# Memory products scaled after the product, the rotary tables an FFN earlier, and another order of the latent panels

## The reference

```python
def memory_attention(q_mem, mem, mem_norm_g, w_mem_kv, g_q, g_k):
    q = rms_norm(q_mem.reshape(b, s, MEM_HEADS, MEM_HEAD_DIM), g_q)
    k, v = jnp.split(rms_norm(mem, mem_norm_g) @ w_mem_kv, 2, axis=-1)
    k = rms_norm(k.reshape(b, m, MEM_HEADS, MEM_HEAD_DIM), g_k)
    ...softmax(q k / 8) v...

for layer in range(2):
    if layer == 1:
        shared = shared_mla_kv(x, ...)          # latent keys and values, rotary key
    x = x + 0.5 * swiglu(rms_norm(x, norm_g[layer, 0]), ...)
    h = rms_norm(x, norm_g[layer, 1])
    # layer 0: short convolution, three gates; layer 1: mla_queries and causal attention
    x = x + concatenate([y_mix, memory_attention(...)]) @ w_out[layer]
    x = x + 0.5 * swiglu(rms_norm(x, norm_g[layer, 2]), ...)
```

## Time and profile before

| | us |
|---|---|
| median of the runs | 3041.64 (3040.64 to 3044.88) |
| the profiled execution | 3040.4 |
| its span | 3038.2 |
| TensorE busy | 2986.5 (98%) |
| VectorE busy | 1828.8 (60%) |
| ScalarE busy | 943.8 (31%) |
| GpSimd busy | 231.7 (8%) |

### The profile page before, as it was taken

The page is one execution under the profiler, slowest core; times in us unless marked ns, Lnnn a source line. Parts: engine busy times, 40 slices in busy tenths (PEclk is TensorE's granted clock), DMA queues, the critical chain, the costliest instruction groups (busy, mean ns, idle before and its releaser), DMA issues.

```text
span 3038.2 us, 36195 instructions
## 1 busy us (share of the span) xinstructions
PE 2986.5 (98%) x13373; PEld 2418.5 (80%) x13373; DVE 1828.8 (60%) x2405; ACT 943.8 (31%) x1279; POOL 231.7 (8%) x107
## 2 busy tenths in 40 slices
PE   8999999999999999999999999999999998999999
PEld 7787788788888887888787888887888875688887
DVE  8896565567766546554587655446554467665532
ACT  4643632333222222222223222222222235322222
POOL 0043240000000000000032000002000022000000
PEclk9999999999999999999999999999999999999999
DMA  4222223233322222223332222332223321122232
GB/s 146 97 93 81 68 97 117 67 103 105 97 97 97 97 97 88 96 95 105 113 107 70 90 97 97 104 104 95 92 97 104 104 87 63 35 90 97 97 104 97
DMA packets 79305, 287.55 MB, mean 95 GB/s; under 512 B 8992, under 2 KB 9248, under 8 KB 78816
## 3 DMA queue, kind: packets, MB, share of 16 engines
q1 hardware_dynamic: 77904, 280.06, 27.5%
q0 software_dynamic: 1296, 6.03, 0.6%
HBM read 283.96 MB, written 2.10 MB: 94 GB/s over the span
## 4 chain that ended last, share of the span: by engine, by line
PE 83%; issue 10%; DVE 5%; POOL 2%; ACT 1%; DMA 0%; POOLq 0%; ACTq 0%; DVEq 0%
PE ps L663 26%; PE ps L665 26%; PE ps L664 26%; POOL w_lo L622 2%; PE ps L1052 1%; PE ps L1297 0%; DVE w_lo L1846 0%; PE ps L1260 0%; DMA mem_x<-in_mem 0%; ACT w_hi L1344 0%; PE ps L833 0%; PE ps L727 0%; PE ps L1041 0%; DVE small L1997 0%; PE ps L947 0%
## 5 line engine op out<-in xcount | busy, mean ns | idle before, releaser
L1344 ACT ACTIVATE w_hi<-raw 128x1024 fp32r<-128x1024 f32 x524 | 554.4, 1058 | 1385.7 <-PE ps L665 1383.5
L663 PE MATMUL ps<-h_hi,w_hi 128*128 128x512 f32 (+1 forms) x2379 | 935.1, 393 | 8.7 <-DVE w_lo L1846 3.3
L665 PE MATMUL ps<-h_hi,w_lo 128*128 128x512 f32 (+1 forms) x2379 | 924.3, 389 | 0.0
L664 PE MATMUL ps<-h_lo,w_hi 128*128 128x512 f32 (+1 forms) x2379 | 924.3, 389 | 0.0
L1846 DVE TENSOR_TENSOR w_lo<-raw,w_hi 128x1024 fp32r<-128x1024 f32 x434 | 530.7, 1223 | 473.9 <-ACT w_hi L1344 473.1
L663 PEld LDWEIGHTS ps<-h_hi,w_hi 128*128 128x128 f32 x2379 | 448.4, 188 | 115.7 <-issue 13.5
L665 PEld LDWEIGHTS ps<-h_hi,w_lo 128*128 128x128 f32 x2379 | 447.8, 188 | 93.0
L664 PEld LDWEIGHTS ps<-h_lo,w_hi 128*128 128x128 f32 x2379 | 448.2, 188 | 92.0 <-issue 2.6
L663 PE MATMUL ps<-mid_hi,w_hi 128*128 128x512 f32 x1208 | 470.8, 390 | 2.2 <-DVE mid_lo L1924 2.1
L664 PE MATMUL ps<-mid_lo,w_hi 128*128 128x512 f32 x1208 | 470.0, 389 | 0.0
L665 PE MATMUL ps<-mid_hi,w_lo 128*128 128x512 f32 x1208 | 470.0, 389 | 0.0
(11 more groups left out here) (409 smaller groups left out, 2471.7 us busy)
## 6 DMA issues: line engine op xcount, KB each, us to landing
raw<-in_wstream SPq DMA_DIRECT2D x525, 512.0 KB, 3.3
x<-in_x SPq DMA_DIRECT2D x4, 512.0 KB, 7.1
x_in<-in_x POOLq DMA_DIRECT2D x8, 256.0 KB, 3.2
mem_x<-in_mem POOLq DMA_DIRECT2D x2, 1024.0 KB, 5.1
out<-x SPq DMA_DIRECT2D x8, 256.0 KB, 4.5
tmp<-in_ret_decay POOLq DMA_DIRECT2D x1, 1024.0 KB, 5.0
rope_r<-in_rope_r POOLq DMA_DIRECT2D x1, 512.0 KB, 3.7
mats<-in_mats SPq DMA_DIRECT2D x1, 256.0 KB, 8.4
```

The source lines that it names most:

```text
L663: nc.tensor.matmul(dst, hi_w, hi_x, start=first, stop=False)
L664: nc.tensor.matmul(dst, hi_w, lo_x, start=False, stop=False)
L665: return nc.tensor.matmul(dst, lo_w, hi_x, start=False, stop=last)
L1344: nc.scalar.activation(w_hi[:, n % HL], raw[:, r], ACT.Copy).then_inc(hi_ready, 1)
```

## The change

1. The root of `mem` is applied behind the product: the halves are made of `mem` times its gain alone, the high one by ScalarE (`memory_hi`), the low one by VectorE (`memory_lo`, one step for a tile). In layer 0 VectorE drains the four memory tiles with a product with the root's reciprocal (`memory_drain`); in layer 1 ScalarE still drains them and VectorE scales them in place (`memory_scaled`).
2. The squares of `mem` are one ScalarE instruction, their sum one `tensor_reduce` of VectorE.
3. In norm round 0 the three scalings stand ahead of the tap `conv_part(st, 3, 1, 3)`.
4. The positions are loaded right behind `mem_x`, before GpSimd's run `conv0`; the rotary tables are computed by VectorE behind the first two units of `s0b_in`, and the Sin stands behind the Silus of `s0b_in`.
5. Latent order: the sums of `cq` stand behind the fourth panel of `mla_in`; the first two memory panels come first in `uq`, the query panel with one tile (number 4) before number 3; rounds 3 to 6 and the rotations move with them; the last round is spread behind the first scores.

```diff
-MEM1_PANEL, MEM1_TILE = (2, 3, 7, 8), (10, 11, 17, 18)
-UQ_PANEL, UQ_TILE = (0, 1, 4, 5, 6), (2, 3, 6, 7, 12, 13, 14, 15, 16)
-V_TILE = (0, 1, 4, 5, 8, 9)
+MEM1_PANEL, MEM1_TILE = (0, 1, 7, 8), (2, 3, 17, 18)
+UQ_PANEL, UQ_TILE = (2, 3, 4, 6, 5), (4, 5, 8, 9, 12, 13, 15, 16, 14)
+V_TILE = (0, 1, 6, 7, 10, 11)
...
@@ GpSimd @@
             pool.dma_start(mem_x[:], A["mem"]).then_inc(side_loaded, 16)
             pool.wait_ge(side_loaded, 48)
+            pool.dma_start(krope[:, 0].bitcast(I32), A["positions"].to_broadcast([P, S])).then_inc(side_loaded, 16)
+            pool.wait_ge(side_loaded, 64)
             split_run("conv0")
...
             pool.dma_start(mem_x1[:], A["mem"]).then_inc(side_loaded, 16)
-            pool.wait_ge(side_loaded, 64)
-            pool.dma_start(rope2[:, 0].bitcast(I32), A["positions"].to_broadcast([P, S])).then_inc(side_loaded, 16)
             pool.wait_ge(side_loaded, 80)
...
@@ TensorE, mla_in, ukv, uq @@
+                if j == 3:
+                    sums("cq")
...
                 if g == 0:
-                    sums("cq")
-                if g == 1:
                     spread_norms("cq")
...
             v_turned_tiles(0)
-            uq_gemm(0)
+            mem1_gemm(0)
+            mem1_gemm(1)
             round_spread(1)
             round_sums(2)
+            uq_gemm(0)
             v_turned_tiles(2)
+            round_spread(2)
+            round_sums(3)
             uq_gemm(1)
-            round_spread(2)
             v_turned_tiles(4)
-            mem1_gemm(0)
-            mem1_gemm(1)
+            round_spread(3)
+            turn(krope[:, 0])
             uq_gemm(2)
-            round_sums(3)
+            uq_gemm(4)
+            round_sums(4)
             uq_gemm(3)
-            round_spread(3)
-            round_sums(4)
-            uq_gemm(4)
             round_spread(4)
             round_sums(5)
-            turn(krope[:, 0])
             mem1_gemm(2)
+            normalised(4)
+            turn(q_rope[:, 0])
             round_spread(5)
             round_sums(6)
-            normalised(4)
-            turn(q_rope[:, 0])
             mem1_gemm(3)
-            round_spread(6)
-            memory_turned(st.t + MEM1_TILE[2] + 1, mem_vt1, 0)
...
             pair_scores(0)
             pair_scores(1)
-            memory_turned(st.t + MEM1_TILE[3] + 1, mem_vt1, 1)
+            round_spread(6)
+            for j in range(2):
+                memory_turned(mem_vt1, j, (mem_scaled, 3 + j))
...
@@ ScalarE @@
+                if n == ST["conv0"].n + 2:
+                    act.wait_ge(side_loaded, 48)
+                    nc.scalar.activation(mem_squares, mem_x[:], ACT.Square).then_inc(mem_squared, 1)
+                if n == ST["conv0"].n + 3:
+                    memory_hi(0, mem_x, mem_hi)
...
-            ffn("s0b")
+            silus("s0b_in", root)
+            act.wait_ge(sin_in, 2)
+            nc.scalar.activation(rope2, rope2, ACT.Sin).then_inc(sin_done, 1)
+            gemm("s0b_out", to_stage("s0b_out"), parts=3)
...
             v_copies(0)
-            uq_drain(0)
+            mem1_drain(0)
+            mem1_drain(1)
+            act.wait_ge(mem_scaled, 2)
+            round_squares(3, qm[:, 0], qm[:, 1], mem_k1_whole)
             round_root(2)
             aux[0] += 3
+            uq_drain(0)
             v_copies(2)
-            act.wait_ge(h_ready, 5 * DT)
+            round_root(3)
+            aux[0] += 4
             uq_drain(1)
             v_copies(4)
-            mem1_drain(0)
-            mem1_drain(1)
-            drained_up_to(MEM1_TILE[1])
-            round_squares(3, qm[:, 0], qm[:, 1], mem_k1_whole)
+            drained_up_to(UQ_TILE[3])
             uq_drain(2)
-            round_root(3)
-            aux[0] += 3
             drained_up_to(UQ_TILE[4])
             round_squares(4, *(q_rope[:, j] for j in range(3)))
-            uq_drain(3)
+            uq_drain(4)
+            drained_up_to(UQ_TILE[5])
+            round_squares(5, *(q_nope[:, hd] for hd in range(3)))
             round_root(4)
...
@@ VectorE @@
+            def memory_sum():
+                dve.wait_ge(mem_squared, 1)
+                v.tensor_reduce(acc[:, 0:MEM], mem_squares.rearrange("p k n -> p n k"), AX.X, ALU.add).then_inc(acc_ready, 1)
...
+            def memory_lo(l, mem, hi, lo, tiles):
                 for k in tiles:
-                    h = acc[:, MEM * (k % 2):MEM * (k % 2) + MEM]
-                    done(v.scalar_tensor_tensor(out=h, in0=mem[:, k], scalar=vcol("mem_norm_g_2", 8 * l + k),
-                                                in1=r[:, 0:MEM], op0=ALU.mult, op1=ALU.mult))
-                    halves(hi[:, k], lo[:, k], h, h_ready)
+                    dve.wait_ge(mem_cast, 8 * l + k + 1)
+                    v.scalar_tensor_tensor(out=lo[:, k], in0=mem[:, k], scalar=vcol("mem_norm_g_2", 8 * l + k),
+                                           in1=hi[:, k].bitcast(F32), op0=ALU.mult, op1=ALU.subtract).then_inc(h_ready, 1)
+
+            def memory_drain(j):
+                st = ST["mem0"]
+                dve.wait_ge(panel_done, st.n + j + 1)
+                dst = mem_k[:, j] if j < 2 else mem_vt[:, j - 2]
+                v.tensor_tensor(dst, bank(st.t + j)[:, 0:MEM], mem_root, ALU.mult).then_inc(drained, 1)
+
+            def memory_scaled(j):
+                dve.wait_ge(drained, ST["uq"].t + MEM1_TILE[j] + 1)
+                tile = mem_k1[:, j] if j < 2 else mem_vt1[:, j - 2]
+                v.tensor_tensor(tile, tile, mem_root, ALU.mult).then_inc(mem_scaled, 1)
...
-            conv_part(st, 3, 1, 3)
             round_norms(*memory_gain("q", 0), qm[:, 0], qm[:, 1])
             round_norms(*memory_gain("k", 0), mem_k_whole)
+            conv_part(st, 3, 1, 3)
...
+            def rotary_tables(c):
+                if c == 0:
+                    dve.wait_ge(side_loaded, 64)
+                    done(v.tensor_copy(angle, krope[:, 0].bitcast(I32)))
+                    done(v.tensor_scalar(angle, angle, vcol("inv_freq", 0), None, ALU.mult))
+                    rotary_table(0, 0.25)
+                if c == 1:
+                    rotary_table(1, 0.0)
+
+            ffn("s0b", gain2(1, 0), behind=rotary_tables)
...
+            memory_lo(1, mem_x1, mem1_hi, mem1_lo, range(4, 8))
             round_reciprocal(1)
-            memory_input(1, mem_x1, spare[:, 0], mem1_hi, mem1_lo, range(4, 8))
+            for j in range(2):
+                memory_scaled(j)
             round_norms(gk, *(k_nope[:, hd] for hd in range(3)))
```

More of the change, by code:

```diff
@@ L382, in build @@
         rope_in = [cpad[:, 0, 4:], cpad[:, 1, 4:], stage[:, 0], stage[:, 1]]
+        rope2, angle, turns = cpad[:, :, 4:], ckv[:, 0], ckv[:, 1]
         ret_out = [[stage[:, 0], stage[:, 1]], [cpad[:, 0, 4:], cpad[:, 1, 4:]]]
@@ L387, in build @@
         mem1_hi, mem1_lo = by_token(h_hi[:, 4:8]), by_token(h_lo[:, 4:8])
-        mem_k1, mem_v1 = (spare[:, j].rearrange("p (a n) -> p a n", n=MEM) for j in range(2))
-        mem_k_whole, mem_k1_whole = mem_k[:].rearrange("p a n -> p (a n)"), spare[:, 0]
+        mem_v1 = spare[:, 1].rearrange("p (a n) -> p a n", n=MEM)
+        mem_k_whole, mem_k1_whole = (k[:].rearrange("p a n -> p (a n)") for k in (mem_k, mem_k1))
+        mem_root = spare[:, 0, 0:MEM]
         mem_vt1 = rstd[:].rearrange("p (a n) -> p a n", n=MEM)
@@ L1697, in _ @@
                     root()
-                if n == ST["conv1"].n:
-                    memory_root(spare[:, 0])
-            def memory(l, k, v_in):
-                st = ST[f"mem{l}"]
-                for j in range(4):
-                    split(st.n + j + 1)
-                    if j == 0:
-                        act.wait_ge(drained, st.t)
-                    drain(st.n + j, st.t + j, k[:, j] if j < 2 else v_in[:, j - 2], cols=MEM)
-            memory(0, mem_k, mem_vt)
+                if n == ST["conv0"].n + 2:
[3 more added lines that the diff above has]
+                    memory_hi(0, mem_x, mem_hi)
+                if n == ST["conv1"].n:
+                    memory_root()
+            for j in range(4):
+                split(ST["mem0"].n + j + 1)
             act.wait_ge(drained, ST["mem0"].t + 2)
@@ L2541, in _ @@
                 scaled(ST["qm0"].n + j, ST["qm0"].t + j, qm[:, j])
-            memory_rms(r)
-            memory_input(0, mem_x, r, mem_hi, mem_lo, range(0, 4))
+            memory_rms()
+            memory_lo(0, mem_x, mem_hi, mem_lo, range(0, 4))
             conv_part(ST["conv1"], 2, 0, 2)
-            memory_input(0, mem_x, r, mem_hi, mem_lo, range(4, 8))
+            memory_lo(0, mem_x, mem_hi, mem_lo, range(4, 8))
             conv_part(ST["conv1"], 2, 1, 2)
@@ L2570, in _, with rotary_table @@
             x_gemm("wo0", residual(1.0, "wo0", gain2(0, 2)), 3)
-            ffn("s0b", gain2(1, 0))
+            magic = 1.5 * 2.0 ** 23
+            c1 = 6.28125
+            c2 = float(np.float32(np.round((2 * np.pi - c1) * 2.0 ** 20) / 2.0 ** 20))
+            c3 = 2 * np.pi - c1 - c2
```

(25 more changed lines are left out.)

87 lines of the change are left out of this document (33 added, 54 removed).

## The result

The changed kernel takes 3048.9 us (median of 12 runs, 3044.3 to 3050.7) against 3041.7 us of the kernel before beside it (12 runs, 3039.6 to 3044.9). The ratio is 1.0019, 95% interval 1.0011 to 1.0028, so 5.8 us slower (3.3 to 8.5); it is the ratio of the means, and the medians are 7.2 us apart. The twelve times stand in two groups with nothing between: five from 3044.3 to 3045.1, seven from 3048.9 to 3050.7. The profiled execution, 3044.5 us, is of the lower one.

The account below looks back on a forecast made before the run. TensorE, busy 2986.5 of 3038.2 us, was taken as the bound. The terms 5.0 + 7.5 - 3.65 - 4.8 - 4.7 = -0.65, from the median 3041.6, gave 3041.0 us, range 3033 to 3048.5.

Parts of the forecast that it names:

- A: conv0: GpSimd waits at once for the positions' load before its low halves; 5.0 us slower, ends 2 and 5.8.
- B: s0b: rotary tables on VectorE delay its low halves, two waits of TensorE; 7.5 us slower, ends 5.5 and 10.
- C: First memory product: VectorE reaches the panels in time but for 0.95 us; 3.65 us faster, ends 1.5 and 4.9.
- E: MLA stage: 14.5 us of losses go, 9.8 of new waits come; 4.7 us faster, ends 0 and 12.2.
- D: First norm round: scaling ahead of a tap removes TensorE's wait for mem_k; 4.8 us faster, ends 3 and 5.
- E's first wait: MLA stage, between the two first memory panels: TensorE waits 3.65 us for GpSimd's low half, plus 1.3 of clock.
- F: Rival, MLA stage: weights for the second memory panel and uq panel 3 come in time; 3033.5 us, chance 0.20.
- S: Rival, MLA rounds: VectorE and GpSimd block each other, costing 8 us; 3049 us, chance 0.14.
- N: Rival, first memory product: VectorE still arrives late at the second panel, gain there 0; 3044.7 us, chance 0.08.

Follow-up runs that it names:

- A alone: Kernel before, with only a second load of the positions in front of GpSimd's conv0 run, waited for there: 3048.6 us, ratio 1.0019.

## Why the prediction was wrong

The forecast was 3041.0 with a range up to 3048.5; the median is 3048.9, and slower by more than 0.2% had 0.16 of the chance, within 0.2% 0.62, and the ratio, 1.0019, is at that edge. Of the 7.9 us between forecast and median, 4.7 lie in the profiled execution (3039.8 forecast, 3044.5 measured) and 3.2 between it and the median.

- **The waits: right.** A 3.72 us (forecast 3.72); B 3.58 and 2.37 (3.75 and 2.4); C 0.77 (0.95); the two in front of MLA panels 3.72 and 2.23 (3.65 and 2.55). E's others: 0.78 for the sums (0.5), 1.09 and 0.71 for a reciprocal and the rotation's tile (0.8 and 0.95); unforeseen are 0.78 in front of the last ukv panel and 0.47 at 2561, both for ScalarE's drains. GpSimd's first half in conv0 began at 1517.01.
- **C and D: right in size,** -3.6 and -5.4 in the profile; D was taken back by itself and cost 6.4 us. C wasn't run alone.
- **The step that failed is the price of the clock:** "I price a new wait of over 2.8 us at its length plus 1.3, a shorter one at its length." The waits of 2.37 and 2.23 us, priced at their length, had 1.3 and 1.5 us of half clock behind them; the wait of 1.88 us in front of s1a_out, with none behind it in the trace of before, had 1.1. The long ones had 1.7, 1.7 and 1.5 instead of 1.3. That is 4.9 us of half clock over the forecast, nearly all of the 5.2 by which the profiled span missed the sum; the waits not foreseen and D's better result make up most of the rest. The evidence for "none behind the waits of about 2 us" was one execution of before. In ten of fourteen profiles the 1.9 us of s1a_out are followed by half clock, and that trace was one of the four others. The size was misread too: 2.05 is half of a window whose granted clock was 0.58, so by that clock 1.7 us were lost in it.
- **A second term was too small, the step from the profile to the median.** The forecast added 1.2 us from the profiled execution to the median; for the changed kernel it is 4.4. Before has its runs spread over 3038 to 3045; the changed kernel has seven of twelve 4.4 to 6.2 us above its profile. One program profiled in both of its groups shows these to be half clock behind unchanged waits. No profile of the changed kernel itself fell in its upper group, so for it that is argued from the other program, and from the mean granted clock of its runs: 0.995 in the lower group, 0.993 in the upper. The version without the wait in conv0 was profiled in its upper group: ahead of conv0, where it is the same program, it falls back against after by 1.7 us at 1145 and 1.6 at 1172. The version with the tables in s1a_in0 has both stretches in a run of its lower group, so these two places alone don't make the groups.
- **Prices taken singly on the chip:** A 5.8 to 6.7 us, B 8, D 6.4, E's first wait 5.5. Against the waits that went or came (3.2 or 3.8, 6.0, 3.8, 3.0 us) each price is 2 to 3.5 us above the length, with an uncertainty of some 3 to 4 us, that of two ratios.
- **Rivals.** F did not happen, and its opposite, that ScalarE's queue sets the wait, was shown by the order alone (the wait fell from 3.72 to 0.69, the time by 5.5 us). S, at 3049, gave the right time by luck: steps of VectorE are stretched in those rounds as it says (the two scalings of the memory keys took 1.41 us on average, the two others 0.42), but no wait that the forecast had there is longer than forecast by more than 0.3. N falls.
- The Trainium skill (SBUF — State Buffer, "Who interferes with whom") lets GpSimd hold back steps of VectorE that read two SBUF inputs. The trace agrees: in the version with tables in s1a_in0 such a step took 2.71 us where it takes 0.69 alone. The step behind it, with one SBUF tile for input, took 2.62 where its fellow took 0.48, so both kinds are held; neither ended a wait of TensorE.

## What to carry to other kernels

Where one engine is busy 98% of the time and its clock sinks behind its waits, sum up the waits of a change and put half clock behind them as a chance that grows with the length, not only behind those where one trace happens to show it. In the fourteen profiles, past the start of the program, half clock followed all 27 waits of 3.3 us and more, 20 of the 25 of 2.1 to 3.0 us, and 16 of the 30 of 1.85 to 2.1 us. (Many of these are the same wait in several versions.) Where it is measured above it cost 1.1 to 2.8 us. Read the same wait in several executions before a stretch is put down to a change. Work that is given to an engine which feeds a two-buffer ring is free only up to the slack it has within one turn of the ring: cut it into pieces of that size (here three steps a unit: 0.9 us of waits instead of 6.0), for a later place doesn't make it cheaper. Issue a load early, but put the wait for it where its data is used.

## What was not expected of the hardware

- Behind the same wait of 2.06 us TensorE ran on at 2.4 GHz in eight executions and at 1.2 GHz for some 3.4 us in six. Such stretches alone put two executions of one program 5.2 us apart, 3031.5 and 3036.7.
- Behind waits of 2.51, 2.80 and 2.96 us TensorE ran on at full clock as well, in one profile each (two versions above), while it sank behind a wait of 2.96 and one of 2.81 in others.
- A broadcast load of the positions (256 KB), waited for at once, keeps GpSimd from its next work for 3.48 us from its issue in conv0 of the changed kernel, 3.77 in the kernel with A alone and 3.72 in the MLA stage of before.
- A block on VectorE can hold GpSimd's work up with no lock between the two, by way of ScalarE's queue: 8.54 us idle for a Silu, and two high halves behind it.
